# First head's K in the exponentials' buffer, and the loads of K and Q at other places of the queue

## The chip, the cores and the metric

One core of one Trainium2 chip runs the whole kernel. The metric is device time in microseconds (us) of one launch. TensorE (PE in the profile) multiplies, VectorE (DVE), ScalarE (ACT) and GpSimd (POOL) work element by element, and SyncE (SP) only issues transfers (DMAs) between the chip's memory and the on-chip buffer.

## The reference, cut to what matters

One encoder block: a projection of the normalised input, two groups that read it (differential attention with a linear distance bias, and a bidirectional state-space group), an output projection and an MLP. The change lies at the seam between the projection and the attention.

```python
hn = rmsnorm(h, norm1_g[l])
proj = hn @ w_in[l]                       # 2048 x 1024 @ 1024 x 2048
q = proj[..., :ATTN_WIDTH].reshape(bsz, s, ATTN_HEADS, 2, ATTN_QKDIM)
k = proj[..., ATTN_WIDTH:2 * ATTN_WIDTH].reshape(bsz, s, ATTN_HEADS, 2, ATTN_QKDIM)
v = proj[..., 2 * ATTN_WIDTH:3 * ATTN_WIDTH].reshape(bsz, s, ATTN_HEADS, ATTN_VDIM)
u = proj[..., 3 * ATTN_WIDTH:]            # for the state-space group
...
bias = -slopes[:, None, None] * dist[None]            # dist = |qpos - kpos|
sc = jnp.einsum('bqhcd,bkhcd->bhcqk', qi, k) * scale   # c: two score maps
p = jax.nn.softmax(sc + bias[None, :, None], axis=-1)
a = p[:, :, 0] - lam * p[:, :, 1]
return jnp.einsum('bhqk,bkhe->bqhe', a, v)
```

There are 4 heads, 2048 positions, and 64 entries per half of a head's query or key.

## The kernel before

The kernel is written by hand, engine by engine, and its order is the order of the code. Every dependence between engines is a semaphore that one raises and another waits for, and each engine, SP too, takes its instructions strictly in turn. So a wait on an engine holds up all that is written behind it.

**The projection** (`phase_project`) is 64 groups, n = 0 to 63 (`NG` = 64), of 24 matmuls each, 8 groups to a block of positions. Blocks 0 to 3 (n < 32, `SECOND`) make Q and K, blocks 4 to 7 make V (the first four groups of a block, `is_v`) and u (the last four). A group's 512 columns go to one of six accumulator banks. DVE empties Q, K and u groups (`evacuate_qku`) and ACT the V groups (`evacuate_v`). SP then stores each from a double buffer to memory (`store`). Full precision comes from splitting each operand in a rounded part ("hi") and a rest ("lo"), with three products. Beside this, DVE and ACT prepare tables for the state-space group (`SsmPrep`): ACT's last store of them, of `pj_made` to `cp_s`, is issued in step 54.

**The attention** (`Attention`, `phase_attention`) takes 64 tiles of 128 queries, 16 to a head. For a tile PE makes scores in two halves of 1024 keys (`scores(n, 0)`, `scores(n, 1)`, each for two maps c; L1188 multiplies by K hi, L1193 by K lo), DVE adds the bias and keeps the running top (`add_bias`, L1112, `negate_top`, L1119), ACT takes the exponentials (L1065), DVE combines the two maps (`combine`, L1135), PE transposes the result (`turn`, L1207), ACT copies that out (`copy_turned`, L1081), and PE multiplies by V (`values`, L1221).

**The seam.** PE runs the scores of tiles 0 and 1 between the last groups of the projection:

```python
            if n >= NG - 4:
                attention.scores(pe, (n - NG + 4) // 2, n % 2)
```

Before `scores(0, 0)`, after group 60, all this must be there. K of head 0 must be loaded (`load_k`, four transfers of 512 KB, L989), split by ACT in eight pieces (`k_high`, L1041), and its rests made, the first four pieces by DVE (`first_k_low`, L1049) and the last four by POOL (`more_k_low`, L1049). Q of tile 0 must be loaded (`load_q`, two transfers of 64 KB, L980), split by ACT (`q_high`, L1020), and its rest made by POOL in two instructions (`q_low`, L1032). DVE makes the bias table from distances (`biases`, L1155, two instructions) and the two factors of lambda. PE's wait is for `k_lo_ready` and `q_lo_ready`.

The buffers decide how early that can be. In the kernel before, `k_raw` lies where the projection's input `x_raw` lies, so that the load of K waits until the last block of x is split. The buffer of exponentials `e` (slots 0 and 1, by tile) lies where the table preparation has its parameters, columns and a part of `pj_made`; POOL writes the distances into slot 1 (`distance_of`), and `q_raw` lies in `pj_made` too, so that both wait for the store to `cp_s` (`outer_stored`). Q has two slots by tile number, and a load of tile n waits until the rest of tile n-2 is made.

In `phase_attention`, SP loads tile n+2 in step n, so that tiles 2 and 3 come in steps 0 and 1, behind all of the projection's SP program. That program ends with a wait for the landing of all u stores.

Of the kernel before, what the change touches and what calls it, by code (L numbers as in the profile page):

```python
# [22 lines left out]
ACT = mybir.ActivationFunctionType  # L23
# [370 lines left out]
def phase_project(nc, ctx, shared, x_t, norm1_g, w_in, qk_s, v_s, u_s, prep_in, attention_in):  # L394
# [111 lines left out]
    def _(sp):  # L506
# [53 lines left out]
        for n in range(NG):  # L560
            b, g = n // NGROUP, n % NGROUP
            if b and g == 0 and b + 1 < NBLOCK and fresh_x(b + 1):
                load_x(BLOCK_X[b + 1])
            if n in (SECOND - NGROUP, SECOND - NGROUP + 2):
                for piece in range(n - SECOND + NGROUP, n - SECOND + NGROUP + 2):
                    load_w(HALF_W + piece)
            elif SECOND - NV <= n < SECOND:
                load_w(HALF_W + g)
            store(n)
            if n == NG - 8:  # L570

                sp.wait_ge(rinv_ready, NTB)
                sp.wait_ge(stats_done, NTB)
                attention.load_lambda(sp)
                sp.wait_ge(x_hi_ready, KD * (max(BLOCK_X) + 1))
                sp.wait_ge(x_lo_ready, KD * (max(BLOCK_X) + 1))
                sp.wait_ge(squares_ready, NTB)
                prep.all_used(sp)
                for i in range(2):
                    sp.wait_ge(qku_stored[i], 16 * SECOND // 2)  # L580
                attention.load_k(sp, 0)
                sp.wait_ge(prep.outer_stored, 16 * 2 * NQU)
                for tile in range(2):
                    attention.load_q(sp, tile)
            if n == NG - 3:
                sp.wait_ge(group_done, NG - NGROUP + NV)
                for i in range(2):
                    sp.wait_ge(v_stored[i], 16 * NV * NTB // 2)
                attention.load_v(sp, 0)
        for i in range(2):  # L590
            sp.wait_ge(qku_stored[i], 16 * (SECOND + NV * NTB) // 2)

    @block.gpsimd
    def _(pool):
# [41 lines left out]
    def _(act):  # L636
# [58 lines left out]
        for n in range(NGROUP - 1, NG):  # L695
            b, g = n // NGROUP, n % NGROUP
            if g == NGROUP - 1 and b + 1 < NBLOCK and fresh_x(b + 1):
                split_x(b + 1)
            if g == 1 and 0 < b < NTB:
                stats(b)  # L700
            if is_v(n):
                if n == SECOND:
                    act.wait_ge(rinv_ready, NTB)
                evacuate_v(n)
            if SECOND - NGROUP < n <= SECOND:
                split_w(HALF_W + n - (SECOND - NGROUP) - 1)
            if n in PREP_TABLES:
                prep.tables_scalar(act, PREP_TABLES.index(n))
            if n == NG - 7:
                prep.all_used(act)  # L710
                attention.k_high(act, 0, range(4))
            if n == NG - 6:
                attention.q_high(act, 0)
                attention.k_high(act, 0, range(4, 8))
            if n == NG - 5:
                attention.q_high(act, 1)
                attention.exponent_lambda(act)
            if n - 2 in PREP_OUTERS:
                prep.store_outer(act, PREP_OUTERS.index(n - 2))
# [3 lines left out]
    def _(dve):  # L723
# [59 lines left out]
        for n in range(NG):  # L783
# [15 lines left out]
            if SECOND - NGROUP < n <= SECOND:  # L799
                split_w(HALF_W + n - (SECOND - NGROUP) - 1)  # L800
            prepare(n)
            if n == NG - 6:
                attention.first_k_low(dve)
            if n == NG - 5:
                prep.all_stored(dve)
                attention.biases(dve)
                attention.lambda_exponents(dve)
# [13 lines left out]
    def _(pe):  # L821
# [45 lines left out]
                attention.scores(pe, (n - NG + 4) // 2, n % 2)  # L867
        for last in range(NG - 4, NG):
            evacuated(pe, last)
    return block, attention  # L870


class Attention:
# [17 lines left out]
    def __init__(self, nc, m, shared, qk_s, v_s, lam_in, att_s, att_square, att_floor, regions, banks):  # L891
# [3 lines left out]
        keys, wide = (shared.region(nc, "at", *part) for part in ((0, 4 * TB * 2), (shared.LOW, 4 * TB)))  # L895
        u_at = shared.LOW + 2 * shared.TAB + PAIRS * T * GH
        inputs, tabs = (shared.region(nc, "at", *part) for part in ((u_at, 2 * G * NJ), (u_at + 2 * G * NJ, 2 * shared.TAB)))
        self.k_raw = keys.sb("k_raw", [P, 2, S])
        self.k_hi = [r.sb(f"k_hi{i}", [P, 2, S], F32R) for i, r in enumerate((inputs, low))]
        self.k_lo = [r.sb(f"k_lo{i}", [P, S], F32R) for i, r in enumerate((wide, low))]  # L900

# [4 lines left out]
        self.a_t = high.sb("a_t", [P, 2, self.NQ, P])  # L906
        self.bias = tabs.sb("bias", [P, self.STRIP], F16)
        self.e = prep.sb("e", [P, 2, 2, S])
        self.q_raw = prep.sb("q_raw", [P, 2, 2, P])
        self.q_hl = squares.sb("q_hl", [P, 2, 2, P], F32R)  # L910
        self.att = rows.sb("att", [P, 2, self.QB, P])
# [70 lines left out]
    def load_k(self, sp, h):  # L982
        if h:
            self.k_lo_wait(sp, h - 1)
            sp.wait_ge(self.k_hi_ready, 8 * h)
        src = self.qk_s[h + H:h + H + 1].rearrange("o (c d) t -> (o d) c t", c=2)
        for c in range(2):
            for twin in range(2):
                sp.dma_start(self.k_raw[twin * DH:(twin + 1) * DH, c], src[:, c]).then_inc(self.k_loaded, 16)  # L989

    def load_v(self, sp, h):

# [41 lines left out]
    def k_high(self, act, h, pieces):  # L1034

        for i in pieces:
            c, cols = i // 4, slice(i % 4 * TB, (i % 4 + 1) * TB)
            if i == 0:
                act.wait_ge(self.k_loaded, 64 * (h + 1))
                self.wait(act, self.scores_done, 4 * self.NQ * (h - 1))  # L1040
            act.activation(self.k_hi[h % 2][:, c, cols], self.k_raw[:, c, cols], ACT.Copy).then_inc(self.k_hi_ready, 1)  # L1041

    def k_low(self, eng, h, i):


        c, cols = i // 4, slice(i % 4 * TB, (i % 4 + 1) * TB)
        rows = slice(c * DH, (c + 1) * DH)
        eng.wait_ge(self.k_hi_ready, 8 * h + i + 1)
        return eng.tensor_tensor(self.k_lo[h % 2][rows, cols], self.k_raw[rows, c, cols],  # L1049
                                 self.k_hi[h % 2][rows, c, cols].bitcast(F32), ALU.subtract)  # L1050

    def first_k_low(self, dve):
# [171 lines left out]
            last.then_inc(self.pv_done, 1)  # L1224


def phase_attention(block, a, head):

# [6 lines left out]
    def _(sp):  # L1237
        for n in range(NS):
            h, s = n // NQ, n % NQ
            if n + 2 < NS:  # L1240
                a.load_q(sp, n + 2)
            if s == 3 and h + 1 < H:
                a.load_k(sp, h + 1)
            if s == 6 and h + 1 < H:
                a.load_v(sp, h + 1)
            if n >= NS - NQ + 1:
                head.load(sp, n - (NS - NQ + 1))
            if n >= 10 and (n - 10) % QB == 0:
                a.store(sp, (n - 10) // QB)
# [1434 lines left out]
def encoder_block(nc, x_t, norm1_g, w_in, lam_in, s_par, s_d, s_bc, w_glu, b_glu, w_stream, gains, y_t):  # L2684
# [17 lines left out]
    with ExitStack() as kept:  # L2702
# [7 lines left out]
        with ExitStack() as ctx:  # L2710
            head = SsmHead(Memory(nc, ctx, "ss"), shared, bp_s, u_s, tab_s, cp_s)
            with ExitStack() as early:
                block, attention = phase_project(
                    nc, early, shared, x_t, norm1_g, w_in, qk_s, v_s, u_s, (s_par, s_bc, mag, tab_s, bp_s, cp_s),
                    (lam_in, att_s, att_square, att_floor))
                phase_attention(block, attention, head)
            phase_ssm(nc, head, following, mag, s_d, w_glu, b_glu, z_s, ssm_s, att_s, att_square, att_floor, gains, att_t)
        phase_mlp(nc, shared, following, x_t, h_s, hn_s, act_s, w_stream, gains, y_t, hb_stored)

# [29 lines left out]
```

## Time and profile before

| | us |
|---|---|
| median of 3 runs | 2672.96 (2672.41 to 2673.84) |
| the profiled execution's own time | 2665.66 |
| its span, first to last instruction | 2663.5 |
| PE busy in the span | 2548.7 (96%) |
| DVE busy | 2077.4 (78%) |
| ACT busy | 1416.7 (53%) |
| POOL busy | 389.5 (15%) |

The span is the profiler's record of one execution, and that execution's own time stands 2.2 us above it. PE is busy nearly all the time, so a stretch of the span in which it stands still is a stretch that counts. Times of rows are counted from the span's start. The projection runs to 407 us and the attention to 974 us.

### The profile page before, as it was taken

The numbers are of one execution on the slowest core, as the hardware profiler recorded it, in microseconds if no ns is written. First come the engines' busy times: TensorE is split into PE (matmuls) and PEld (weight loads), VectorE is DVE, ScalarE is ACT, GpSimd is POOL, SyncE is SP. The second block draws the span as 40 slices with busy tenths as digits, with TensorE's granted clock in tenths as the row PEclk, the third lists the DMA queues.
The fourth block names the chain that finished last, engine by engine and source line by source line (L and its number), as shares of the span: only waits on it lengthen the run. The fifth ranks groups of instructions, "written<-read, shape, count | busy, mean of one in ns | idle before, by whom it ended". The sixth has DMA issues, their size and how long they took to land.

```text
span 2663.5 us, 32920 instructions
## 1 busy us (share of the span) xinstructions
PE 2548.7 (96%) x12804; PEld 2079.2 (78%) x12804; DVE 2077.4 (78%) x2074; ACT 1416.7 (53%) x1753; POOL 389.5 (15%) x333
## 2 busy tenths in 40 slices
PE   7998999999999988988989999999999999999997
PEld 6886777877787877766777888888887888888886
DVE  5866657999999968766998876777889877678885
ACT  5276626777787762224434666533345565643334
POOL 3410021212121113310434000000014000000003
PEclk9999999999999999998999999999999999999999
DMA  5356542020213119966665554452234664452211
GB/s 187 119 188 221 216 136 72 25 64 26 56 39 89 49 41 255 256 220 245 221 236 202 212 206 186 174 205 106 104 109 159 233 221 174 181 198 95 97 78 63
DMA packets 162714, 397.18 MB, mean 149 GB/s; under 512 B 29568, under 2 KB 87168, under 8 KB 134784
## 3 DMA queue, kind: packets, MB, share of 16 engines
q1 hardware_dynamic: 145856, 319.07, 36.1%
q10 hardware_dynamic: 16704, 76.03, 7.2%
q8 instruction: 101, 1.65, 0.3%
q14 instruction: 53, 0.43, 0.1%
HBM read 270.79 MB, written 122.16 MB: 148 GB/s over the span
## 4 chain that ended last, share of the span: by engine, by line
PE 45%; DVE 3%; POOL 1%; issue 1%; DMA 0%; ACT 0%; SPq 0%; DVEq 0%; ACTq 0%; POOLq 0%
PE ml_bank L2590 15%; PE ml_bank L2592 15%; PE ml_bank L2591 15%; POOL kp_tabs L2199 1%; DVE ml_res L2470 1%; DMA kp_low<-hn_s 0%; DVE ml_hb L2504 0%; DVE ml_b_split L2401 0%; DVE ml_w_split L2412 0%; DVE ml_res L2490 0%; DVE ml_rinv L2496 0%; PE ml_bank L2598 0%; DVE kp_low L2425 0%; DVE kp_tabs L2446 0%; DVE ml_t_first L2419 0%
## 5 line engine op out<-in xcount | busy, mean ns | idle before, releaser
L2590 PE MATMUL ml_bank<-ml_b_split,ml_w_split 128*128 128x512 f32 x2016 | 788.8, 391 | 9.7 <-issue 9.4
L2591 PE MATMUL ml_bank<-ml_b_split,ml_w_split 128*128 128x512 f32 x2016 | 786.1, 390 | 0.0
L2592 PE MATMUL ml_bank<-ml_b_split,ml_w_split 128*128 128x512 f32 x2016 | 785.9, 390 | 0.0
L2590 PEld LDWEIGHTS ml_bank<-ml_b_split,ml_w_split 128*128 128x128 f32 x2016 | 379.5, 188 | 93.2 <-issue 14.1
L2591 PEld LDWEIGHTS ml_bank<-ml_b_split,ml_w_split 128*128 128x128 f32 x2016 | 379.6, 188 | 79.9 <-issue 1.2
L2592 PEld LDWEIGHTS ml_bank<-ml_b_split,ml_w_split 128*128 128x128 f32 x2016 | 379.6, 188 | 79.1
L1065 ACT ACTIVATE at_e<-at_e,at_neg_top 128x2048 f32<-128x2048 f32 x128 | 256.5, 2004 | 143.2 <-DVE at_neg_top L1119 143.2
L2199 POOL TENSOR_TENSOR kp_tabs<-kp_tabs,ml_square 128x512 f32<-128x512 f32 x55 | 144.2, 2622 | 1265.8 <-ACT ml_square L2303 1259.3
L2470 DVE TENSOR_TENSOR ml_res<-ml_bank,ml_res 128x2048 f32<-128x2048 f32 x75 | 171.5, 2287 | 118.7 <-PE ml_bank L2592 118.7
L2237 ACT ACTIVATE ml_b_split<-kp_u_t 128x2048 fp32r<-128x2048 f32 x54 | 103.5, 1917 | 300.5 <-PE ml_bank L2592 300.5
L1221 PEld LDWEIGHTS pj_banks<-at_v,at_a_t 128*128 128x128 f32 x2048 | 238.6, 192 | 22.8 <-issue 22.6
L1221 PE MATMUL pj_banks<-at_v,at_a_t 128*128 128x128 f32 x2048 | 255.9, 278 | 0.0
L2401 DVE TENSOR_TENSOR ml_b_split<-kp_low,ml_b_split 128x2048 fp32r<-128x2048 f32 x54 | 123.5, 2287 | 105.1 <-ACT ml_b_split L2237 105.1
L1112 DVE CUSTOM_DVE_ANT_0 at_e<-pj_banks,at_bias,at_top 128x1024 f32<-128x1024 f32 x128 | 164.3, 1284 | 29.3 <-PE pj_banks L1193 26.9
L2237 ACT ACTIVATE ml_b_split<-kp_low 128x2048 fp32r<-128x2048 f32 x54 | 103.4, 1915 | 155.3 <-PE ml_bank L2592 148.2
L1112 DVE CUSTOM_DVE_ANT_0 at_e<-pj_banks,at_bias 128x1024 f32<-128x1024 f32 x128 | 151.6, 1222 | 29.8 <-issue 21.0
L850 PE MATMUL pj_banks<-pj_x_hi,pj_w_hi 128*128 128x512 f32 x384 | 153.1, 399 | 16.3 <-DVE pj_x_lo L733 14.7
L1135 DVE SCALAR_TENSOR_TENSOR at_e<-at_e,at_coef 128x1024 f32<-128x1024 f32 x128 | 164.8, 1289 | 2.3
L1188 PE MATMUL pj_banks<-at_k_hi,at_q_hl 128*128 128x512 f32 x512 | 153.4, 419 | 13.7 <-POOL at_q_hl L1032 6.2
L2401 DVE TENSOR_TENSOR ml_b_split<-kp_u_t,ml_b_split 128x2048 fp32r<-128x2048 f32 x54 | 123.4, 2285 | 50.2 <-ACT ml_b_split L2237 50.2
L1032 POOL TENSOR_TENSOR at_q_hl<-at_q_raw,at_q_hl 64x128 fp32r<-64x128 f32 x128 | 86.4, 675 | 483.7 <-ACT at_q_hl L1020 478.6
L851 PE MATMUL pj_banks<-pj_x_lo,pj_w_hi 128*128 128x512 f32 x384 | 150.7, 392 | 0.0
(227 smaller groups left out, 4057.3 us busy)
## 6 DMA issues: line engine op xcount, KB each, us to landing
act_s<-ml_res ACTq DMA_DIRECT2D x32, 1024.0 KB, 4.2
kp_wide<-in_w_stream SPq DMA_DIRECT2D x18, 1024.0 KB, 5.1
kp_bp<-in_w_stream SPq DMA_DIRECT2D x18, 1024.0 KB, 5.8
kp_tabs<-in_w_stream SPq DMA_DIRECT2D x18, 1024.0 KB, 6.7
ml_r<-in_w_stream SPq DMA_DIRECT2D x18, 1024.0 KB, 6.8
tab_s<-kp_tabs ACTq DMA_DIRECT2D x32, 512.0 KB, 3.0
kp_low<-hn_s SPq DMA_DIRECT2D x16, 1024.0 KB, 5.6
kp_u_t<-hn_s SPq DMA_DIRECT2D x16, 1024.0 KB, 4.8
```

What stands on the lines that cost most here:

```text
L1065: act.activation(self.e[:, n % 2, c], self.e[:, n % 2, c], ACT.Exp, bias=self.neg_top[:, n % 2, c:c + 1], scale=self.SCALE, accum_out=self ...
L1112: dve.tensor_tensor_reduce(out=self.e[:, s % 2, c, half * self.HALF:(half + 1) * self.HALF], in0=self.score[:, c], in1=self.bias[:, at:at ...
L1135: dve.scalar_tensor_tensor(self.e[:, slot, 0, cols], self.e[:, slot, 1, cols], self.coef[:, 1:2], self.e[:, slot, 0, cols], ALU.mult, ALU. ...
L1188: pe.matmul(self.score[:, c, bank * TB:(bank + 1) * TB], self.q_hl[:, n % 2, c], self.k_hi[h % 2][:, c, keys], start=True, stop=False)
L1221: last = pe.matmul(self.pv[:, n % 2, 0:P], self.a_t[:, n % 2, kt], self.v[h % 2][kt], start=(kt == 0), stop=(kt == self.NQ - 1))
L2199: pool.tensor_tensor(sums[:, t], sums[:, t], square[:, done % 2], ALU.add).then_inc(added, 1)
L2237: act.activation(b_split[:, g % 2, 0], raw_b(k, i)[:], ACT.Copy).then_inc(b_hi_ready, 1)
L2401: dve.tensor_tensor(b_split[:, g % 2, 1], raw_b(k, i)[:], b_split[:, g % 2, 0].bitcast(F32), ALU.subtract)\
L2470: dve.tensor_tensor(flat(res[reg]), flat(bank(k, i)), flat(res[reg]), ALU.add).then_inc(dve_left, 1)
L2590: pe.matmul(out, w_hi[:, w], b_hi[:, b], start=fresh and kt == 0, stop=False, skip_group_check=True)
L2591: pe.matmul(out, w_hi[:, w], b_lo[:, b], start=False, stop=False, skip_group_check=True)
L2592: last = pe.matmul(out, w_lo[:, w], b_hi[:, b], start=False, stop=kt == 3, skip_group_check=True)
```

## The change

Four edits, all in the order of things:

1. **K of head 0 goes to slot 0 of `e`** (`k_raw[0]`), no longer to the place of x. Its load needs only that the table preparation has been computed, and is written behind `store(53)` (`NG - 11`) where it was behind `store(56)` (`NG - 8`). The loads of lambda's inputs and of Q of tiles 0 and 1 come along. The waits for x go to the end of the program, since later heads' K still goes to the place of x.
2. **ACT splits all of it in step 55** (`NG - 9`): Q of tile 0, K's eight pieces, Q of tile 1, in one run ahead of `evacuate_v` of 56 to 59. Before, they stood in steps 57, 58 and 59 between those.
3. **DVE** makes the first rests, the bias and the factors of lambda in step 57, before in steps 58 and 59. Nothing else stands between them on DVE.
4. **SP loads Q of tiles 2 and 3 in step 62**, between `store(62)` and `store(63)`, and the wait for the u stores' landing goes to tile 50 of the attention, where u is first read.

```diff
             store(n)
-            if n == NG - 8:
+            if n == NG - 11:
                 sp.wait_ge(rinv_ready, NTB)
                 sp.wait_ge(stats_done, NTB)
                 attention.load_lambda(sp)
-                sp.wait_ge(x_hi_ready, KD * (max(BLOCK_X) + 1))
-                sp.wait_ge(x_lo_ready, KD * (max(BLOCK_X) + 1))
-                sp.wait_ge(squares_ready, NTB)
                 prep.all_used(sp)
...
                 attention.load_k(sp, 0)
                 sp.wait_ge(prep.outer_stored, 16 * 2 * NQU)
                 for tile in range(2):
                     attention.load_q(sp, tile)
+            if n == NG - 2:
+                for tile in range(2, 4):
+                    attention.load_q(sp, tile)
...
-        for i in range(2):
-            sp.wait_ge(qku_stored[i], 16 * (SECOND + NV * NTB) // 2)
+        sp.wait_ge(x_hi_ready, KD * (max(BLOCK_X) + 1))
+        sp.wait_ge(x_lo_ready, KD * (max(BLOCK_X) + 1))
+        sp.wait_ge(squares_ready, NTB)
...
-            if n == NG - 7:
+            if n == NG - 9:
                 prep.all_used(act)
-                attention.k_high(act, 0, range(4))
+                attention.q_high(act, 0)
+                attention.k_high(act, 0, range(8))
+                attention.q_high(act, 1)
             if n == NG - 6:
-                attention.q_high(act, 0)
-                attention.k_high(act, 0, range(4, 8))
-            if n == NG - 5:
-                attention.q_high(act, 1)
                 attention.exponent_lambda(act)
...
-            if n == NG - 6:
+            if n == NG - 7:
                 attention.first_k_low(dve)
-            if n == NG - 5:
                 prep.all_stored(dve)
                 attention.biases(dve)
                 attention.lambda_exponents(dve)
...
-        self.k_raw = keys.sb("k_raw", [P, 2, S])
+        later_k = keys.sb("k_raw", [P, 2, S])
...
+        self.k_raw = [self.e[:, 0]] + [later_k] * (H - 1)
...
-            if n + 2 < NS:
+            if 2 <= n < NS - 2:
                 a.load_q(sp, n + 2)
...
+            if n == NS - NQ + 2:
+                u_written(sp)
```

On SP's queue this moves the rows so. `u_s` and `v_s` are the projection's stores (of groups 52 to 55, then 56 to 59, and so on), `at_k_raw` or `at_e` the load of K, `at_v_54` that of V of head 0. Before, from group 52 on:

```order
L546 DMA u_s<-pj_qku_out 1024x1x64 x4
L538 DMA v_s<-pj_v_out 128x512
L966 DMA at_lam_v<-in_lam 128x256
L989 DMA at_k_raw<-qk_s 64x2048 x4
L980 DMA at_q_raw<-qk_s 64x2x128 x4
L538 DMA v_s<-pj_v_out 128x512 x3
L546 DMA u_s<-pj_qku_out 1024x1x64 x2
L996 DMA at_v_54<-v_s 128x4x128 x4
L546 DMA u_s<-pj_qku_out 1024x1x64 x2
L1236 UNCONDITIONAL_BRANCH
L980 DMA at_q_raw<-qk_s 64x2x128 x8
```

And in the changed kernel:

```order
L546 DMA u_s<-pj_qku_out 1024x1x64 x2
L971 DMA at_lam_v<-in_lam 128x256
L994 DMA at_e<-qk_s 64x2048 x4
L985 DMA at_q_raw<-qk_s 64x2x128 x4
L546 DMA u_s<-pj_qku_out 1024x1x64 x2
L538 DMA v_s<-pj_v_out 128x512 x4
L546 DMA u_s<-pj_qku_out 1024x1x64 x2
L1001 DMA at_v_54<-v_s 128x4x128 x4
L546 DMA u_s<-pj_qku_out 1024x1x64
L985 DMA at_q_raw<-qk_s 64x2x128 x4
L546 DMA u_s<-pj_qku_out 1024x1x64
L1241 UNCONDITIONAL_BRANCH
```

The nine transfers behind group 56's store now stand behind group 53's, ahead of the stores of 54 and 55, and four of the Q loads stand ahead of the last u store and of the branch into the attention.

On ACT, from the last store of the tables (`cp_s`) on, before:

```order
L337 DMA cp_s<-pj_made 128x2304
L648 ACTIVATE pj_x_hi<-kp_low,pj_gain 128x512 x8
L675 ACTIVATE pj_v_out<-pj_banks,pj_rinv_t 128x512 x2
L1041 ACTIVATE at_k_hi_50<-at_k_raw 128x512 x4
L675 ACTIVATE pj_v_out<-pj_banks,pj_rinv_t 128x512
L1020 ACTIVATE at_q_hl<-at_q_raw 128x256
L1041 ACTIVATE at_k_hi_50<-at_k_raw 128x512 x4
L675 ACTIVATE pj_v_out<-pj_banks,pj_rinv_t 128x512
L1020 ACTIVATE at_q_hl<-at_q_raw 128x256
L1070 ACT_TABLE_LOAD
L1070 ACTIVATE at_lam_e<-at_lam_e 128x2
```

And in the changed kernel:

```order
L337 DMA cp_s<-pj_made 128x2304
L649 ACTIVATE pj_x_hi<-kp_low,pj_gain 128x512 x8
L1025 ACTIVATE at_q_hl<-at_q_raw 128x256
L1046 ACTIVATE at_k_hi_50<-at_e 128x512 x8
L1025 ACTIVATE at_q_hl<-at_q_raw 128x256
L676 ACTIVATE pj_v_out<-pj_banks,pj_rinv_t 128x512 x3
L1075 ACT_TABLE_LOAD
L1075 ACTIVATE at_lam_e<-at_lam_e 128x2
L676 ACTIVATE pj_v_out<-pj_banks,pj_rinv_t 128x512
```

The four emptyings of V groups 56 to 59 (`pj_v_out`) now stand behind the ten splits. On DVE, POOL and PE the instructions stand in the same order as before; on DVE only the waits ahead of them differ in what else they pass.

## Rows read from the trace of the kernel before

**Rows 1.** Timeline of TensorE: start us, length us, line, tiles, count, [idle before]

```profile
382.08 2.04 PE L1188 MATMUL pj_banks<-at_k_hi,at_q_hl 128*128 128x512 f32 x4 [6.10 <-POOL at_k_lo L1049]
...
390.81 1.07 PE L1188 MATMUL pj_banks<-at_k_hi,at_q_hl 128*128 128x512 f32 x4
...
392.48 0.50 PE L850 MATMUL pj_banks<-pj_x_hi,pj_w_hi 128*128 128x512 f32 x1
...
414.40 2.08 PE L1188 MATMUL pj_banks<-at_k_hi,at_q_hl 128*128 128x512 f32 x4 [6.19 <-POOL at_q_hl L1032]
...
421.11 1.18 PE L1188 MATMUL pj_banks<-at_k_hi,at_q_hl 128*128 128x512 f32 x4
422.22 0.73 PE L1193 MATMUL pj_banks<-at_k_lo,at_q_hl 64*128 64x512 f32 x4
422.88 2.05 PE L1221 MATMUL pj_banks<-at_v,at_a_t 128*128 128x128 f32 x16
```

**Rows 2.** Busy time by stretch (A:B, length, engines, granted clock, DMA share, GB/s)

```profile
382.00:385.20 3.20, 3.12 (x8) 1.67 (x8) 0.00 (x0) 0.00 (x0) 0.90 (x2) 0.50 0.00 0
...
414.40:421.10 6.70, 6.70 (x32) 5.21 (x33) 3.26 (x8) 5.33 (x9) 0.48 (x2) 0.62 0.08 22
421.10:430.00 8.90, 8.90 (x67) 7.15 (x66) 7.50 (x14) 5.36 (x7) 1.29 (x1) 1.00 0.63 147
```

**Rows 3.** Timeline of POOL ahead of the two stretches

```profile
371.39 5.02 POOL L1032 TENSOR_TENSOR at_q_hl<-at_q_raw,at_q_hl 64x128 fp32r<-64x128 f32 x2 [18.90 <-ACT at_q_hl L1020]
376.49 5.44 POOL L1049 TENSOR_TENSOR at_k_lo<-at_k_raw,at_k_hi 64x512 fp32r<-64x512 f32 x4
...
413.37 0.98 POOL L1032 TENSOR_TENSOR at_q_hl<-at_q_raw,at_q_hl 64x128 fp32r<-64x128 f32 x2 [30.32 <-ACT at_q_hl L1020]
```

**Rows 4.** Timeline of ACT

```profile
368.14 2.19 ACT L1041 ACTIVATE at_k_hi<-at_k_raw 128x512 fp32r<-128x512 f32 x4 [7.75 <-DMA at_k_raw<-qk_s]
...
412.88 0.42 ACT L1020 ACTIVATE at_q_hl<-at_q_raw 128x256 fp32r<-128x256 f32 x1 [14.52 <-DMA at_q_raw<-qk_s]
413.20 1.99 ACT L1065 ACTIVATE at_e<-at_e,at_neg_top 128x2048 f32<-128x2048 f32 x1
...
415.19 1.06 ACT L1081 ACTIVATE at_a_t<-pj_banks 128x512 f32<-128x512 f32 x2
```

**Rows 5.** SP's queue: its timeline, and one row of its waits

```profile
345.08 2.08 SPq L546 DMA_DIRECT2D u_s<-pj_qku_out  x2
...
356.09 2.43 SPq L989 DMA_DIRECT2D at_k_raw<-qk_s  x4
...
399.43 7.77 SPq L546 DMA_DIRECT2D u_s<-pj_qku_out  x2
409.76 13.88 SPq L980 DMA_DIRECT2D at_q_raw<-qk_s  x8
...
SPq L591 <- DMA u_s<-pj_qku_out: 2.3, 1, 2.3
```

**Rows 6.** Transfers: a stretch while K loads; queue 10 (ACT) in 342 to 352 us

```profile
362.00:368.10 6.10, 6.10 (x28) 5.07 (x27) 0.00 (x0) 0.00 (x0) 0.00 (x0) 1.00 1.03 218
...
q10 hardware_dynamic: 144, 1.18, 29.6%
```

**Rows 7.** Timeline of DVE

```profile
368.81 2.49 DVE L1049 TENSOR_TENSOR at_k_lo<-at_k_raw,at_k_hi 64x512 fp32r<-64x512 f32 x4 [16.33 <-ACT at_k_hi L1041]
371.22 4.34 DVE L1155 SCALAR_TENSOR_TENSOR at_bias<-at_e 128x2048 f16<-128x2048 int32 x2
...
408.78 1.28 DVE L1112 CUSTOM_DVE_ANT_0 at_e<-pj_banks,at_bias,at_top 128x1024 f32<-128x1024 f32 x1
```

**Rows 8.** TensorE's clock behind a longer and a shorter idle stretch

```profile
303.42 0.76 PE L845 MATMUL pj_banks<-pj_w_hi,pj_x_hi 128*128 128x512 f32 x1 [2.50 <-DVE pj_x_lo L733]
...
1387.39 0.47 PE L2590 MATMUL ml_bank<-ml_b_split,ml_w_split 128*128 128x512 f32 x1 [1.55 <-issue]
...
1387.40:1390.00 2.60, 2.60 (x12) 2.14 (x13) 2.60 (x5) 2.20 (x2) 0.00 (x0) 1.00 1.05 323
```

More of the change, by code:

```diff
@@ L869, in _, with u_written @@
             evacuated(pe, last)
-    return block, attention
+    def u_written(eng):
+        for i in range(2):
+            eng.wait_ge(qku_stored[i], 16 * (SECOND + NV * NTB) // 2)
+    return block, attention, u_written
 class Attention:
@@ L988, in load_k @@
             for twin in range(2):
-                sp.dma_start(self.k_raw[twin * DH:(twin + 1) * DH, c], src[:, c]).then_inc(self.k_loaded, 16)
+                sp.dma_start(self.k_raw[h][twin * DH:(twin + 1) * DH, c], src[:, c]).then_inc(self.k_loaded, 16)
     def load_v(self, sp, h):
@@ L1040, in k_high @@
                 self.wait(act, self.scores_done, 4 * self.NQ * (h - 1))
-            act.activation(self.k_hi[h % 2][:, c, cols], self.k_raw[:, c, cols], ACT.Copy).then_inc(self.k_hi_ready, 1)
+            act.activation(self.k_hi[h % 2][:, c, cols], self.k_raw[h][:, c, cols], ACT.Copy).then_inc(self.k_hi_ready, 1)
     def k_low(self, eng, h, i):
@@ L1048, in k_low @@
         eng.wait_ge(self.k_hi_ready, 8 * h + i + 1)
-        return eng.tensor_tensor(self.k_lo[h % 2][rows, cols], self.k_raw[rows, c, cols],
+        return eng.tensor_tensor(self.k_lo[h % 2][rows, cols], self.k_raw[h][rows, c, cols],
                                  self.k_hi[h % 2][rows, c, cols].bitcast(F32), ALU.subtract)
@@ L1224, in values, with phase_attention @@
             last.then_inc(self.pv_done, 1)
-def phase_attention(block, a, head):
+def phase_attention(block, a, u_written, head):
     NQ, NS, QB = a.NQ, a.NS, a.QB
@@ L2712, in encoder_block @@
             with ExitStack() as early:
-                block, attention = phase_project(
+                block, attention, u_written = phase_project(
                     nc, early, shared, x_t, norm1_g, w_in, qk_s, v_s, u_s, (s_par, s_bc, mag, tab_s, bp_s, cp_s),
                     (lam_in, att_s, att_square, att_floor))
-                phase_attention(block, attention, head)
+                phase_attention(block, attention, u_written, head)
             phase_ssm(nc, head, following, mag, s_d, w_glu, b_glu, z_s, ssm_s, att_s, att_square, att_floor, gains, att_t)
```

## The prediction

> **What bounds the kernel now.** The page's busy times come first: PE works 2548.7 of 2663.5 us, so what counts is where it stands still. The timeline of TensorE over the seam then shows two stretches [rows 1]. The first, 6.10 us, ends at 382.08 before `scores(0, 0)`, released by POOL's last rest of K. The second, 6.19 us, ends at 414.40 before `scores(2, 0)`, released by POOL's rest of Q of tile 2. Both cost more than their idle time, since the clock is low behind them: 0.50 in 382 to 385.2 and 0.62 in 414.4 to 421.1, and 1.00 from 421.1 on, where PE is busy 8.90 of 8.90 us [rows 2]. From 421.11 each tile of attention follows at PE's own pace. So whatever is won ahead of it moves all the rest of the kernel forward.
>
> Going back along the first wait: POOL's four rests of K end at 381.93 [rows 3]. They wait behind two rests of Q that take 5.02 us beside DVE's bias, where the same pair takes 0.98 later [rows 3, 7]. All of it hangs on ACT's first piece of K at 368.14, released by the load [rows 4], issued from 356.09 on [rows 5]. Going back along the second: POOL's pair at 413.37 follows ACT's `q_high` at 412.88, which waited 14.52 us for its load [rows 3, 4]. That load is issued only at 409.76, behind the last u store and 2.3 us of waiting for its landing [rows 5].
>
> **Part one: the first stretch.** PE is through with group 60 at 382.08 - 6.10 = 375.98. What must be worked out is when K, Q and their rests are ready in the changed kernel.
>
> The load. SP issues `store(53)` at 345.08 [rows 5]. With that issue (about 0.5) and lambda's (about 0.4), K's first transfer goes out at about 346.1, where it was 356.09: 10 us earlier. Before, ACT had K at 368.14, 12.05 us after the first issue. In that time the engines moved K (2.10 MB), Q (0.26 MB) and one V store (0.26 MB), 2.62 MB, at 218 GB/s and a full share [rows 6]: 12.0 us. So it is bandwidth alone. Now K and Q share with the `cp_s` store (2.96 us of all 16 engines, 29.6% of 10 us [rows 6]) and with `store(53)` (0.26 MB, 1.2 us). How much of `cp_s` is left at 346.1 no row says; it is between nothing and all 2.96 us. K and Q are then in at 346.1 + (0 to 2.96) + 1.2 + 2.36 MB / 218 GB/s (10.8) = 358.1 to 361.1. I take T = 360.3, near the late end, since the store is issued only in the step before. V stores don't compete: ACT is held until K is there.
>
> The Trainium skill ("DMA: Bandwidth & Descriptors", section on queues, rings and completion order) has each engine go round between queues by packets. By it `cp_s` lands some 2 us later than alone and so do the issues of Q behind it, but the sum of bytes and T stay. A strict order of queues would give the same T.
>
> The chain behind T. Before, from 368.14 to PE's start at 382.08 it took 13.94 us [rows 1, 4]: four pieces on ACT (2.19), DVE's four rests (to 371.30), its bias (4.34, to 375.56), POOL's blocked pair, and POOL's four rests (5.44) [rows 3, 4, 7]. Now Q's split of 0.4 comes first and the V emptying of 0.6 in the middle is gone; POOL's pair can run before DVE's bias begins, but its rests of K fall beside it, and I let them be blocked in its place. So again 13.9: ready at 374.2 (375.0 for the late T). Were nothing blocked, POOL could end at T + 0.4 + 5 x 0.55 + 5.44 = T + 8.6, or 368.9. Either lies ahead of 375.98, by 1 to 7 us. The first stretch goes, 6.10 us, and with it the low clock: `scores(0, 0)` and its end took 3.12 us of PE [rows 2] and the same warm takes 392.48 - 390.81 = 1.67 [rows 1], so 1.45. **Term one: 7.55 us.**
>
> The Trainium skill ("SBUF — State Buffer", section on the two sides of SBUF) has the port pair of DVE and POOL as an exclusive lock, held also by a DVE instruction with two on-chip inputs while POOL reads there. The trace agrees (5.02 against 0.98 us). By that rule T + 13.9 is the case, and by free running T + 8.6; the sum is the same by both.
>
> What this part could hurt: ACT is held at `q_high(0)` from its last split of x until T, and then for ten splits (8 x 0.55 + 2 x 0.4 = 5.2) to 365.5. The V groups 56 to 58, done meanwhile, wait in their banks. PE needs the bank of 56 for group 62 (after 377) and those of 58 and 59 only for the scores at 375.98, and ACT empties each in 0.6, so nothing waits. The factor of lambda is ready behind the bias at T + 9.1 = 369.4, ahead of `evacuate_v(59)` at 370.4. SP's stores of 54 and 55 go out up to 6 us later; their buffers are next wanted by groups 60 and 61. DVE has no other work between its emptying of groups 55 and 60. These cost 0.
>
> **Part two: the second stretch.** All up to the last projection group moves with term one: the turn that ends at 414.40 - 6.19 = 408.21 now ends at 400.66. `store(62)` goes out at 399.43 - 7.55 = 391.9, Q's first pair by 393.7, landed some 2.5 us later (issue at 409.76, two issues of 0.6, ACT at 412.88: 1.9 [rows 4, 5]), so by 396.2. ACT is idle there and POOL needs 0.98: Q of tile 2 is ready at about 397.7, 3 us early.
>
> Something else is late next. `scores(2, 0)` writes the banks that DVE reads for tile 1. DVE's last `add_bias` of tile 1 ends at 408.78 + 1.28 = 410.06 [rows 7], now 402.51. The first map's half can run before, the second then needs about 0.5, and the products with K lo 0.73 [rows 1]: 403.75. The turn waits for ACT, whose exponential of tile 1 no longer waits for Q (413.20 before, although the top stood ready when DVE began its next instruction at 408.78 [rows 4, 7]). It runs from 401.2 to 403.2 (1.99 [rows 4]), and two copies (1.06) end at 404.3. The turn's second part takes 0.5, the 16 products with V 2.0 [rows 1]: `scores(2, 1)` starts at 406.8. Before it was 421.11. So 12.90 us from 408.21 become 6.14. **Term two: 6.75 us.** If it ran with no wait at all (1.9 for the scores, 2.0 for the products [rows 1], about half as much for the turn: 4.7), it would be 8.2. If the clock fell, PE would lose again what it lost before, about 2.3 us (6.70 us at 0.62, at the low level a matmul takes twice as long): 4.4. A stop of 2.50 us was followed by a slow matmul (0.76 against 0.39), one of 1.55 by a clock of 1.00 [rows 8]. The stops here are about 1.1 and 0.3, so I keep it at full.
>
> **Part three: the rest.** The Q loads of tiles 4 on, K of later heads and the state-space loads stand behind the same events as before, and move with them. The wait for u's landing at tile 50 is long met. 0.
>
> **The sum.** 7.55 + 6.75 = 14.3 us off the profiled execution's own 2665.66: 2651.4. The median of the runs stands 7.3 above that execution. The seam's waits are no part of that difference that I can see, so the same 14.3 comes off 2672.96: **2658.7 us**, 0.53% faster.
>
> **Rivals.**
> *K comes later than T = 362.* If K, Q, `cp_s` and the store disturb each other, every microsecond beyond 362.0 (375.98 - 13.94) is paid. Against it: before, K came in at the engines' full share with V's store beside it [rows 6], so the mixture costs no more than its bytes. With T at 365, 3 us and up to 1.45 for the clock are lost: 2663. Chance 8%.
> *Q of tile 2 is not in time.* Then the second stretch stays. Q now stands behind the V load (1 MB) and a u store; a 3 us margin speaks against it. Only term one: 2665.4. Chance 6%.
> *No gain.* Both waits only change their name, for instance because DVE's bias also delays POOL's pair, and ACT's late V emptying stops PE. Within 5 us of 2673. Chance 5%.
> *Slower.* The two stretches also gave DVE and ACT a lead when tile 2 began. If tiles from 2 on start closer behind them and PE then waits in each of 62 tiles, 14.3 / 62 = 0.23 us a tile eats the gain, and 0.4 a tile gives 2683. For it: DVE is busy 7.50 of 8.90 us in that stretch. Against it: that leaves 1.4 us a tile, in which a lag is made up. Chance 3%.
>
> **How the numbers follow.** The forecast (both stretches go) has 78%, and lies between 2656.5 (term two without any wait, and 0.7 for the spread of the runs) and 2661.7 (low clock in the second, 2.3, and the spread). The range runs to 2666.0, over the two rivals that keep part of the gain. 0.2% is 5.3 us, about what a measurement of this kernel tells from none. Faster by more: 78 + 8 + 5 of 6 for Q = 91%, within: 6%, slower: 3%.
>
> **What would show it.** In the changed profile: K's issue at about 346 and ACT's first split at about 360; POOL's last rest of K before 376; no idle time of PE before `scores(0, 0)`, and 1.7 us for it; `scores(2, 0)` at about 401 with a wait for DVE, not POOL; the step from `scores(2, 1)` to `scores(3, 1)` still 8.9. The prediction is wrong if ACT's first split comes after 362, if PE stops for ACT's `evacuate_v`, or if the pace of the tiles changes.

## The result and the profile after

The changed kernel took 2654.82 us in the median of 4 runs (2649.54 to 2655.98), the kernel before 2672.68 (4 runs, 2667.49 to 2673.84). Three of those four are the runs that the forecast started from; the one new run took 2667.49. The ratio is 0.9933, with a 95% interval of [0.9914, 0.9952]: faster, by 17.9 us where 14.3 were forecast, and 1.7 us below the forecast range. The profiled execution took 2649.54 us with a span of 2647.6.

The page of the changed kernel (engine, busy us, share of the span, instructions): PE has lost 2.9 us of busy time, and nothing else moved by more than 1.6. The matmuls that ran at the low clock before are shorter now.

```profile
PE 2545.8 (96%) x12804; PEld 2078.4 (79%) x12804; DVE 2079.0 (79%) x2074; ACT 1416.6 (54%) x1753; POOL 390.6 (15%) x333
```

TensorE's timeline over the seam, the rows that answer to [rows 1]:

```profile
376.78 1.07 PE L1193 MATMUL pj_banks<-at_k_hi,at_q_hl 128*128 128x512 f32 x4
377.78 0.73 PE L1198 MATMUL pj_banks<-at_k_lo,at_q_hl 64*128 64x512 f32 x4
378.44 0.50 PE L848 MATMUL pj_banks<-pj_x_hi,pj_w_hi 128*128 128x512 f32 x1
...
400.34 1.07 PE L1212 MATMUL pj_banks<-at_ident,at_e 128*128 128x128 f32 x8
401.89 0.70 PE L1193 MATMUL pj_banks<-at_k_hi,at_q_hl 128*128 128x512 f32 x2 [0.48 <-DVE at_top L1117]
403.32 0.73 PE L1193 MATMUL pj_banks<-at_k_hi,at_q_hl 128*128 128x512 f32 x2 [0.72 <-DVE at_top L1117]
403.98 0.73 PE L1198 MATMUL pj_banks<-at_k_lo,at_q_hl 64*128 64x512 f32 x4
404.70 1.09 PE L1212 MATMUL pj_banks<-at_ident,at_e 128*128 128x128 f32 x8
405.63 1.95 PE L1226 MATMUL pj_banks<-at_v,at_a_t 128*128 128x128 f32 x16
407.33 1.17 PE L1193 MATMUL pj_banks<-at_k_hi,at_q_hl 128*128 128x512 f32 x4
```

`scores(0, 0)` at 376.78 has no idle time ahead of it any more, and takes 1.66 us to the next matmul of the projection. `scores(2, 0)` runs in two halves, each released by DVE's reading of tile 1's banks (`at_top`), with stops of 0.48 and 0.72 us in place of one of 6.19. The granted clock stays at its upper level through both places, and from `scores(2, 1)` on the pace is 8.89 us a tile, as in [rows 2]:

```profile
376.70:378.45 1.75, 1.75 (x11) 0.92 (x9) 1.35 (x3) 0.00 (x0) 0.00 (x0) 1.00 0.00 0
400.34:407.33 6.99, 5.79 (x40) 4.36 (x41) 6.53 (x13) 5.37 (x7) 0.00 (x0) 1.00 0.23 59
407.33:416.22 8.89, 8.89 (x68) 7.16 (x66) 8.07 (x17) 6.34 (x10) 1.31 (x2) 1.00 0.47 117
```

SP's queue (the places of [rows 5]) issues lambda's input, K and Q behind `store(53)`, and Q of tiles 2 and 3 at 393.19:

```profile
346.03 0.52 SPq L546 DMA_DIRECT2D u_s<-pj_qku_out  x1
346.64 1.45 SPq L971 DMA_DIRECT2D at_lam_v<-in_lam  x1
348.29 2.94 SPq L994 DMA_DIRECT2D at_e<-qk_s  x4
351.27 2.69 SPq L985 DMA_DIRECT2D at_q_raw<-qk_s  x4
...
393.19 2.66 SPq L985 DMA_DIRECT2D at_q_raw<-qk_s  x4
```

ACT's first split is the time T of the prediction:

```profile
361.82 0.42 ACT L1025 ACTIVATE at_q_hl<-at_q_raw 128x256 fp32r<-128x256 f32 x1 [11.31 <-DMA at_q_raw<-qk_s]
362.14 4.26 ACT L1046 ACTIVATE at_k_hi<-at_e 128x512 fp32r<-128x512 f32 x8
...
371.54 0.69 ACT L676 ACTIVATE pj_v_out<-pj_banks,pj_rinv_t 128x512 f32<-128x512 f32 x1
...
396.50 0.42 ACT L1025 ACTIVATE at_q_hl<-at_q_raw 128x256 fp32r<-128x256 f32 x1 [4.93 <-DMA at_q_raw<-qk_s]
```

DVE makes its four rests and then the bias:

```profile
362.79 2.76 DVE L1054 TENSOR_TENSOR at_k_lo<-at_e,at_k_hi 64x512 fp32r<-64x512 f32 x4 [9.37 <-ACT at_k_hi L1046]
365.48 4.35 DVE L1160 SCALAR_TENSOR_TENSOR at_bias<-at_e 128x2048 f16<-128x2048 int32 x2
```

POOL's last rests of K, beside that bias, end at 375.35, 1.43 us before PE comes to them:

```profile
362.41 1.39 POOL L1037 TENSOR_TENSOR at_q_hl<-at_q_raw,at_q_hl 64x128 fp32r<-64x128 f32 x2 [8.97 <-ACT at_q_hl L1025]
364.99 10.36 POOL L1054 TENSOR_TENSOR at_k_lo<-at_e,at_k_hi 64x512 fp32r<-64x512 f32 x4 [1.19 <-ACT at_k_hi L1046]
...
397.00 1.07 POOL L1037 TENSOR_TENSOR at_q_hl<-at_q_raw,at_q_hl 64x128 fp32r<-64x128 f32 x2 [20.52 <-ACT at_q_hl L1025]
```

### The profile page after: what moved, and what is told of

Same layout as the page of the kernel before. It is cut to its first block, busy times and chain, and to the rows that moved or that the text cites. A ratio compares the mean times of both kernels' runs of the same rounds, so it can differ in the third digit from the quotient of the medians.

```text
span 2647.6 us, 32919 instructions
## 1 busy us (share of the span) xinstructions
PE 2545.8 (96%) x12804; PEld 2078.4 (79%) x12804; DVE 2079.0 (79%) x2074; ACT 1416.6 (54%) x1753; POOL 390.6 (15%) x333
## 4 chain that ended last, share of the span: by engine, by line
PE 45%; DVE 3%; POOL 1%; DMA 1%; issue 1%; ACT 0%; SPq 0%; DVEq 0%; ACTq 0%; POOLq 0%
PE ml_bank L2597 15%; PE ml_bank L2599 15%; PE ml_bank L2598 15%; POOL kp_tabs L2206 1%; DMA kp_low<-hn_s 0%; DVE ml_res L2477 0%; DVE ml_b_split L2408 0%; DVE ml_hb L2511 0%; DVE ml_w_split L2419 0%; DVE ml_res L2497 0%; DVE ml_rinv L2503 0%; DMA ml_hb<-h_s 0%; PE ml_bank L2605 0%; DVE kp_low L2432 0%; DVE kp_tabs L2453 0%
```

## The experiments

The theory after the result: the seam gives what was forecast, 14 to 15 us, and the rest of the 17.9 is scatter between runs and between profiles. The rival: something further on also became faster. Second question: how much margin the new order has, and who uses it up.

### The same kernels again (e1, e2, e10)

No edit: the changed kernel twice more and the kernel before once more, each timed.

> The changed kernel once more. My theory (seam and chance): the gain that the change makes is 14.5 us at the seam, in every execution, and what the first timing showed beyond it (17.9 us in all) is scatter of waits for transfers in the state-space stage. Then five rounds give a gain of 14.5 us with a scatter of some 2 us (12.5 to 16.5), and the state-space stage, from its first transposes to the MLP's first matmul, was 249.5 us in the profile of before and 247.5 us in that of after, takes either length in either kernel. Rival (a second gain): the change also shortens the state-space stage, each time, by about 2 to 3.5 us. Then the gain is again 17 to 18 us and the stage is again near 247.5 us here and near 249.5 us in the kernel before.

> The kernel before, unchanged, timed against itself: 0 us of difference, and its scatter is the size below which nothing is to be read. Seam and chance: its state-space stage can come out anywhere from 247 to 250 us. A second gain: it is near 249.5 us again.

> The changed kernel itself beside the one with the early bias, for the comparison and for the spread of medians. Theory, the seam gains 14.5 to 15 us and the rest is the scatter of the runs: ratio 0.9935 to 0.9955, runs spread over 6 to 9 us, the profiled execution's stage of the diagonal products anywhere between 244 and 255 us. Rival, the first median of 2654.82 was the kernel's own and the second, 2655.99, the exception: ratio below 0.9935 again.

Measured, each against the kernel before of the same comparison. Gains in microseconds are the ratio applied to the median of the kernel before.

| | median us (runs, from to) | the kernel before | ratio |
|---|---|---|---|
| changed, first | 2654.82 (4, 2649.54 to 2655.98) | 2672.68 (4, 2667.49 to 2673.84) | 0.9933 [0.9914, 0.9952] |
| changed, again (e1) | 2655.99 (5, 2649.92 to 2658.50) | 2668.72 (20, 2665.45 to 2673.58) | 0.9945 [0.9933, 0.9958] |
| changed, third (e10) | 2655.58 (6, 2652.35 to 2657.82) | 2667.91 (11, 2663.47 to 2672.40) | 0.9952 [0.9940, 0.9964] |
| before, again (e2) | 2667.84 (11, 2664.69 to 2671.93) | 2668.72 (20) | 0.9994 [0.9986, 1.0003] |

The changed kernel repeats within 1.2 us. Its gain is 14.7 us in e1, where 14.5 was expected and the rival had 17 to 18, and 12.8 in e10, whose ratio lies in the expected 0.9935 to 0.9955. What moved is the kernel before: of the 42 later runs of it (20, 11 and 11) 3 lie at 2672.4 or above, and so did all three that the forecast started from, which are also three of the four in the first row. Its mean over the 42 is 2668.7, that of the changed kernel over its 15 runs is 2654.7: 13.9 us.

The profiles show where runs of one kernel differ. Each is cut at five landmarks on TensorE's timeline: the first matmul of the projection's block 6 (the one with 2.50 us of idle time ahead of it), `scores(2, 1)`, the first transposes of the state-space stage (`sm_turn_ps`), the first matmul of the MLP (`ml_bank`), and the end. Microseconds:

| | start to block 6 | block 6 to `scores(2, 1)` | attention | state space | MLP | span |
|---|---|---|---|---|---|---|
| before | 303.42 | 117.69 | 566.57 | 249.47 | 1426.35 | 2663.5 |
| before, again | 303.41 | 118.06 | 566.71 | 247.04 | 1427.68 | 2662.9 |
| changed | 304.47 | 102.86 | 566.47 | 247.46 | 1426.34 | 2647.6 |
| changed, again | 304.82 | 102.99 | 566.73 | 247.17 | 1426.29 | 2648.0 |
| changed, third | 304.88 | 102.99 | 566.73 | 252.60 | 1428.20 | 2655.4 |

The second column holds the seam. It is the same to 0.4 us in runs of one kernel, and differs by 14.9 between the kernels (117.88 against 102.95 in the mean). The first column takes 1.3 us of that back: it is 303.4 us in both profiles of the kernel before and 304.1 to 305.1 in all ten profiles of kernels with an edit, though no instruction ahead of block 6 was changed. The cause is open. So 13.6 us are left at `scores(2, 1)`, against the 13.9 of the timed means. The attention is the same in all. (In the kernel before its last matmul ends at 983.9 us; the 974 given ahead of the prediction is too early.) The state-space stage varies by 5.6 us and the MLP by 1.9 with nothing changed. The rival of a second gain falls. For the third run of the changed kernel, the first part of the state-space stage (windows: stretch, length, busy time of PE, PEld, DVE, ACT, POOL, clock, DMA share, GB/s):

```profile
974.60:1155.60 181.00, 161.27 (x768) 131.76 (x769) 135.57 (x228) 40.33 (x95) 58.98 (x54) 0.93 0.88 227
```

and the same part of its first profile:

```profile
974.50:1150.50 176.00, 157.81 (x768) 129.66 (x768) 136.75 (x229) 40.49 (x95) 58.69 (x49) 0.96 0.88 235
```

The same 768 matmuls take 3.5 us more of busy time at a clock of 0.93 in place of 0.96, the idle time is 1.5 us longer, and in both the DMA engines are 88% busy. TensorE's waits for loads in the stage, in total, times, longest. Third profile:

```profile
PE sm_y_ps L1822 <- DMA sm_toeplitz<-sm_strip: 4.4, 3, 2.8
...
PE sm_lag_ps L1798 <- DMA kp_low<-cp_s: 1.2, 1, 1.2
PE sm_lag_ps L1798 <- DMA sm_cp<-cp_s: 1.1, 1, 1.1
```

First profile:

```profile
PE sm_turn_ps L1785 <- DMA kp_bp<-bp_s: 2.4, 1, 2.4
...
PE sm_y_ps L1822 <- DMA sm_toeplitz<-sm_strip: 1.6, 3, 0.8
...
PE sm_lag_ps L1798 <- DMA kp_low<-cp_s: 0.4, 1, 0.4
```

The sums are 6.7 and 4.4 us. They do not give the stage's length by themselves: the second profile of the kernel before has 6.6 us of such waits and a stage of 247.04. So the scatter sits in a stage whose loads keep the engines nearly full, and shows there mostly as matmuls at the lower clock. That the place of the stops decides the clock is a guess; no run tested it.

### One half of the change at a time (e3, e4)

K only, that is the changed kernel without edit 4:

```diff
-            if n == NG - 2:
-                for tile in range(2, 4):
-                    attention.load_q(sp, tile)
...
+        for i in range(2):
+            sp.wait_ge(qku_stored[i], 16 * (SECOND + NV * NTB) // 2)
...
-            if 2 <= n < NS - 2:
+            if n + 2 < NS:
```

Q only is the kernel before with edit 4, so the same lines the other way round.

> Only the first three edits: K into slot 0 of e behind group 53, the splits in step 55, the bias in step 57. The loads of Q of tiles 2 and 3 stay behind the projection's last stores. Seam and chance: 7.5 us faster than before (7 to 8.5, with the scatter 5.5 to 9.5), the first stop of TensorE gone and the second still there with about 6 us. A second gain, if it hangs on the first three edits: 10 to 11 us, and the state-space stage near 247.5.

> Only the fourth edit: Q of tiles 2 and 3 in step 62, and the wait for the u stores at tile 50. K is loaded as before. Seam and chance: 7.0 us faster than before (with the scatter 5 to 9), the first stop of 6.1 us still there, the second down to two short waits for VectorE. A second gain, if it hangs on the moved wait for the u stores: 10 us, and the state-space stage near 247.5. If the two parts add, this and the kernel with the first three edits alone sum to the changed kernel's gain.

Measured: K only 2660.62 us (9 runs), ratio 0.9976 [0.9966, 0.9986], 6.4 us where 7.5 were expected; Q only 2660.07 (6 runs), 0.9969 [0.9957, 0.9981], 8.3 us where 7.0 were expected. Both lie in their expected ranges, and the intervals overlap, so the times do not say which half gives more. Block 6 to `scores(2, 1)` takes 109.31 and 110.87 us, so the seam gains 8.6 and 7.0. Each half removes its own stop and leaves the other's. TensorE with K only:

```profile
408.16 2.08 PE L1192 MATMUL pj_banks<-at_k_hi,at_q_hl 128*128 128x512 f32 x4 [6.19 <-POOL at_q_hl L1036]
```

TensorE with Q only:

```profile
383.66 2.05 PE L1193 MATMUL pj_banks<-at_k_hi,at_q_hl 128*128 128x512 f32 x4 [5.96 <-POOL at_k_lo L1054]
```

The halves add up to 15.6 us in the seam, against 14.9 for both together. In the ratios they add up to 14.7, and the changed kernel timed beside them (e1) gains 14.7.

### Only the wait for u's landing moved (e8)

K only once more, with the wait moved to tile 50 but Q of tiles 2 and 3 still loaded in the attention's first steps. It splits the second gain between the wait and the place of the loads.

```diff
-        for i in range(2):
-            sp.wait_ge(qku_stored[i], 16 * (SECOND + NV * NTB) // 2)
...
+            if n == NS - NQ + 2:
+                u_written(sp)
```

> The first three edits, and of the fourth only the wait for the u stores moved to tile 50; Q of tiles 2 and 3 is still loaded in the attention's steps 0 and 1, behind store(63). By my reading of the queue: the wait is 2.2 us, so TensorE's stop before scores(2, 0) falls from 6.2 to about 3.7 us, and the seam from 36.9 to about 34.4 us; the place of the loads then accounts for the other 4 us. Rival (the u store ahead in the queue delays Q by itself): the stop stays near 6 us, because Q's transfers wait behind the store's in the queue anyway.

Measured, one execution: 2662.69 us, of which the profile's state-space stage has 254.65, the longest of all; so the seam is read, not the time. Q is issued at 400.57, where K only issued it at 403.55 behind 2.2 us of waiting (0.7 us of the difference is a projection that was ahead here), and TensorE's stop is 4.14 us, where 3.7 was expected:

```profile
405.43 2.07 PE L1190 MATMUL pj_banks<-at_k_hi,at_q_hl 128*128 128x512 f32 x4 [4.14 <-POOL at_q_hl L1034]
```

The wait is worth the 2.05 us of stop between 6.19 and 4.14, and 1.7 us of time: from the first scores to `scores(2, 1)` it takes 35.2 us, where K only takes 36.9 and 34.4 were expected. The place of the loads, ahead of `store(63)`, takes the stop from there to the 1.20 us of the changed kernel, and the same stretch to 30.6: in the changed kernel Q goes out at 393.19, and SP comes to `store(63)` only at 399.87.

### The loads two steps later (e5)

```diff
-            if n == NG - 11:
+            if n == NG - 9:
```

This tests the chain behind T: K arrives some 6 us later, and the prediction says that all beyond T = 362 is paid.

> The changed kernel with the loads of K and Q written behind group 55's store (the last place at which ACT's order still holds), in place of group 53's. The theory of a deadline: the split of K starts at T = 366 in place of 361.8, POOL's last rest of K ends 13.5 us behind it, at about 379.7, TensorE is ready at about 376.8 and stops for 3 us, and the clock falls or not: the seam, from the first scores to scores(2, 1), is unchanged or up to 1.5 us longer, and the stretch before it 3 us longer than in the changed kernel. Rival (the 4 us of margin that the distance of T to 376.8 seems to leave are still there, since POOL's rests need only 5.4 us once nothing blocks them): no stop.

Measured, one execution: 2662.05 us beside 2665.36 for the kernel before. K goes out at 354.59, ACT begins at T = 368.30, POOL is 10.23 us over its rests:

```profile
371.47 10.23 POOL L1054 TENSOR_TENSOR at_k_lo<-at_e,at_k_hi 64x512 fp32r<-64x512 f32 x4 [1.18 <-ACT at_k_hi L1046]
```

and TensorE's stop is back:

```profile
381.85 2.05 PE L1193 MATMUL pj_banks<-at_k_hi,at_q_hl 128*128 128x512 f32 x4 [5.15 <-POOL at_k_lo L1054]
```

Here POOL is through at T + 13.4 (381.70), and at T + 13.5 in the changed kernel. PE was done with group 60 at 376.70. The stop was expected at 3 us, because T was put at 366. K and Q took as long from their first issue as in the changed kernel (13.7 and 13.5 us), so the 6.3 us of the later issue reached T in full. From block 6 to `scores(2, 1)` it takes 110.27 us: 7.3 of the 14.9 us are lost again, nearly all of term one. The theory of a deadline at about T = 363 stands, and the size was missed with T.

### The bias a group earlier (e6, e9)

The last 13.5 us of the chain hold 4.35 of DVE's bias. The distances are there since POOL's work at 353, so DVE can make it before K comes.

```diff
+            if n == NG - 8:
+                prep.all_stored(dve)
+                attention.biases(dve)
             if n == NG - 7:
                 attention.first_k_low(dve)
-                prep.all_stored(dve)
-                attention.biases(dve)
```

> The changed kernel with DVE's bias made in step 56, while DVE waits for K, and only the rests of K and lambda's factors behind K. Theory (DVE's bias blocks POOL): POOL's four rests of K take about 5.5 to 7 us in place of 10.36 and end near 370 in place of 375.35; TensorE starts its first scores at the same time as in the changed kernel, so the time does not move. Rival (POOL is slow for another reason, its instructions or the transfers): still about 10 us.

> The changed kernel with the bias made a group earlier, timed. Its one profiled execution had the seam of the changed kernel to 0.01 us and no stop; POOL's last rest ended 5.8 us ahead of the first scores of the attention in place of 1.4 us. Theory, the cover is free and was already enough: no gain and no loss, ratio to the kernel before 0.993 to 0.996, median within 1.5 us of the changed kernel's own beside it. Rival, in some of the executions that carry no profile POOL is late in the changed kernel and the stop comes back there: then this kernel is faster than the changed one by 1 to 3 us in the median, and its slowest runs lie lower.

Measured: one execution (e6) 2654.11 us; timed (e9) 2654.79 (6 runs, 2650.77 to 2656.72), ratio 0.9949 [0.9936, 0.9962], beside 2655.58 for the changed kernel (e10). Seam and stops are those of the changed kernel. The 0.8 us between the medians is less than the 1 to 3 us of the rival and well inside the scatter of the runs. In the profile of e6, DVE's bias:

```profile
353.59 4.36 DVE L1161 SCALAR_TENSOR_TENSOR at_bias<-at_e 128x2048 f16<-128x2048 int32 x2
```

and POOL's rests:

```profile
365.11 6.16 POOL L1055 TENSOR_TENSOR at_k_lo<-at_e,at_k_hi 64x512 fp32r<-64x512 f32 x4 [1.12 <-ACT at_k_hi L1047]
```

With no bias beside them they take 6.16 us in place of 10.36; the 4.20 between is nearly the bias's own length, so POOL stood still for it. With K two steps later the same edit gives the same: 10.23 us in e5 and 6.13 in e7, so the time at which K comes is not what makes POOL slow. That agrees with the Trainium skill ("SBUF — State Buffer", section on the two sides of SBUF), by which the engine that comes second waits for the whole instruction of the other. The margin grows from 1.43 to 5.8 us (371.27 against 377.09) and the time stays. So 1.4 us of margin was enough in these runs.

### Both edits (e7)

The loads two steps later and the bias earlier. If only POOL's rests were on the chain, the stop of 5.15 us should shrink to 1 us or less.

> K behind group 55 and the bias in step 56 together. Deadline and block: POOL ends near T + 9.2 = 375.5, before TensorE is through with group 60, so no stop, or one under 1 us, though K comes 4 us later than in the changed kernel. Rival (K's arrival alone decides): the same stop as with K behind group 55 and the bias late.

Measured, one execution: 2656.89 us. POOL is done at 378.25, T + 9.3 as expected, and TensorE with group 60 at 377.48. POOL alone would have stopped it for 0.8 us, but it stops for 1.94, until 379.42, and for another engine. That is neither the stop of under 1 us that was expected nor the rival's 5.15:

```profile
379.42 1.57 PE L1194 MATMUL pj_banks<-at_k_hi,at_q_hl 128*128 128x512 f32 x4 [1.94 <-ACT pj_v_out L676]
```

ACT's timeline shows what is late. The last V emptying (378.65) stands behind one that waits 1.54 us for a store, a table load and lambda's exponential:

```profile
376.54 0.69 ACT L676 ACTIVATE pj_v_out<-pj_banks,pj_rinv_t 128x512 f32<-128x512 f32 x1 [1.54 <-DMA v_s<-pj_v_out]
377.25 1.28 ACT L1076 ACT_TABLE_LOAD   x1
378.54 0.20 ACT L1076 ACTIVATE at_lam_e<-at_lam_e 128x2 f32<-128x2 f32 x1
378.65 0.67 ACT L676 ACTIVATE pj_v_out<-pj_banks,pj_rinv_t 128x512 f32<-128x512 f32 x1
```

A second chain hangs on T, and the first one hid it: ACT's V emptyings end at T + 10.4 (T = 368.95). In the changed kernel the same chain ends at 372.23, also T + 10.4, 4.5 us ahead of PE. Soon behind the stop of 1.94 us the granted clock (third column from the end) was 0.50:

```profile
380.00:383.00 3.00, 3.00 (x9) 1.59 (x8) 0.69 (x1) 0.00 (x0) 0.00 (x0) 0.50 0.59 175
```

## Why the prediction was right in its terms and wrong in its range

**Term one, 7.55 us: right.** The stop of 6.10 us is gone, and `scores(0, 0)` takes 1.66 us where it took 3.12 in [rows 2]: 7.56. The way there had two errors that cancel in part. K's first issue came at 348.29, not 346.1: 0.95 of it is a projection that ran later in this profile (346.03 for `store(53)`, 345.08 in [rows 5]), most of the rest is lambda's issue, which took 1.45 us and not 0.4. K and Q then needed 13.5 us and not 14.2. What that sum was made of was not right, though. The `cp_s` store had landed 4.3 us after its issue at 344.97, only 1.0 us behind K's first issue, and took the same 4.3 us in the kernel before, so it did not land 2 us late. And the stores of groups 54 and 55 went out at 354.01, right behind Q, where the sum had nothing. T less the 0.95 is 360.9, in the range of 358.1 to 361.1. POOL was blocked by the bias as assumed, T + 13.5 against T + 13.9; e6 shows that it was the bias.

**Term two, 6.75 us: right.** The turn ends at 401.41 and `scores(2, 1)` starts at 407.33, 5.92 us later, where it was 12.90: 6.98. DVE is the new waiter, with 1.20 us in two stops (1.4 forecast), and the clock held. Q of tile 2 was ready at 398.07, 3.3 us early. e8 shows that 1.7 us of the term belong to the wait for u's landing.

That each term fits so closely is in part luck, since one profile holds such a term only to about 1.5 us. Behind the first stop the low clock lasted 3.2 us in the first profile of the kernel before and 6.3 in the second. The same stretch in the first:

```profile
385.20:390.80 5.60, 5.60 (x26) 4.67 (x25) 2.38 (x4) 0.00 (x0) 0.00 (x0) 0.99 0.00 0
```

and in the second (e2):

```profile
385.20:390.80 5.60, 5.60 (x19) 4.45 (x20) 2.38 (x4) 0.00 (x0) 0.00 (x0) 0.72 0.00 0
```

Behind the second stop it was the other way round: 12.90 us from the turn to `scores(2, 1)` in the first, 11.99 in the second. Against the second profile the two terms come out at 9.0 and 6.1 us. Their sum is firmer, 14.7 and 15.1 us.

**What was costed at nothing.** The V emptyings, lambda, the later stores and the pace of the tiles cost nothing: the changed kernel has no further stop between block 6 and `scores(2, 1)`, and its attention takes the time of before. The cover for the V emptyings was 4.5 us, and e7 shows the stop that comes when it is used up. The last of them began at 371.54 and not at 370.4: the one ahead of it waited 1.55 us for a store, and the table load for lambda takes 1.28, neither of which the prediction counted. It saw that mechanism only under "no gain".

**The step that failed** is the one from the trace to the median: "the same 14.3 comes off 2672.96", and with it "0.7 for the spread of the runs" at the low end. The sum of 14.3 was 0.6 us below the seam's 14.9 and 0.4 above the 13.9 by which the means of all later runs differ, so the gain was sized well. The miss is the number from which it was taken. The three runs lay within 1.4 us of each other, and were taken for the kernel's time; 42 further runs spread over 10.1 us around 2668.7. 14.3 off that mean is 2654.4, with 2654.7 measured over 15 runs.

The prediction had a hint: its own profiled execution took 2665.66, 7.3 us below the median, and it said only that the seam had no part in this. A hint is all it was. In the seven timings with several runs since then, the profiled execution lay between 6.1 us below and 2.2 above the median, 3.0 below in the mean. But no other gap was as large as 7.3, and 0.7 us for the spread was too little beside it. Why the first three runs lay so close together at the upper edge is open. With 3 of 42 at that height, chance is a poor explanation. The later runs are from two chips, with means of 2668.9 (31 runs) and 2668.1 (11 runs); on which chip the first three ran is not on record.

**The rivals.** K came at 361.8 in a profile whose deadline was 376.78 - 13.5 = 363.3 (the forecast's limit of 362.0 holds for a projection that runs as early as in the first profile); Q of tile 2 was 3.3 us early; the tiles kept their 8.89 us. None of the four came about, though the first was nearer than the forecast had it: 1.4 us.

## What to carry to other kernels

Before a difference is taken off a median, time the unchanged kernel again at another time: a close group of three runs is no spread, and the same three runs in the comparison afterwards make the gain look larger than it is (17.9 us with them here, 13.9 without them). Take the price of a stop from more than one profile, since the time at the low clock behind it varies. When a late arrival is pulled forward, list every chain that hangs on it, not only the one that the profile names, since the second (here ACT's V emptyings, which end 3.1 us ahead of the first) decides as soon as the first is cut by more than that. Halves that each remove their own stop can be tried alone, and here nearly added up.

## What was not expected of the hardware

- Lambda's input on SP took 1.45 us to issue in the changed kernel at 346.64 and 0.61 us in e5, 7 us later. In the changed kernel ACT had issued the `cp_s` store at 344.97, and the DMA engines were 96% busy from 346 to 348. Which of these makes the issue long was not tried.
- K and Q needed 13.5 us from the first issue in the changed kernel, with the last 1.0 us of the `cp_s` store and the stores of groups 54 and 55 beside them, and 13.7 us in e5, with only the store of group 55 gone out just ahead of them. The engines moved 230 GB/s over the first of these stretches and 197 over the second. So the time did not follow the bytes, as the forecast of T had it. Why the transfers were slower in e5 is open.
- Stops of TensorE of 0.48 and 0.72 us left the granted clock at its upper level, 2.4 GHz, and one of 1.94 us was followed by the lower, 1.2 GHz, after 0.6 us of work at the upper one. In [rows 8] a stop of 1.55 us kept the upper level and one of 2.50 did not. The forecast had counted on the clock only for stops up to 1.1 us.
